# A hybrid decoder step on one core: a new opening of the head pairs, block-diagonal chunk states, late top-k rounds and a token-major last norm

## What is computed

```python
n = rmsnorm(x, norm1)
c_rw, c_att, c_gate = _split(n @ w_in, (RW_COLS, ATT_COLS, GATE_COLS))
o_rw, wkv_new, shift_new = rwkv7_mix(c_rw, shift_prev, wkv_prev, ...)
o_att = attend(q, k, v, qi, ki, wi * IDX_W_SCALE)      # top-k indexer, then softmax over the selected keys
merged = jax.nn.sigmoid(g_rw) * (o_rw @ p_rw) + jax.nn.sigmoid(g_att) * (o_att @ p_att)
h = x + merged @ w_o
f, conv_new = conv_glu(rmsnorm(h, norm2), conv_prev, w_up, conv_w, conv_b, w_down)
y = rmsnorm(h + f)                                     # after the last layer
```

## Time and profile before

| | |
|---|---|
| median of 3 runs | 1784.6 us (1784.6 to 1786.84) |
| the profiled execution's own time | 1784.55 us |
| its span, from the first to the last instruction | 1783.0 us |
| PE busy | 1762.4 us, 99% |
| DVE busy | 1119.2 us, 63% |
| ACT busy | 759.8 us, 43% |
| mean share of the DMA engines | 40 to 60% in most slices |
| granted clock of PE, mean | 0.998 |

### The profile page before, as it was taken

The page is one execution under the profiler, slowest core; times in us unless marked ns, Lnnn a source line. Parts: engine busy times, 40 slices in busy tenths (PEclk is TensorE's granted clock), DMA queues, the critical chain, the costliest instruction groups (busy, mean ns, idle before and its releaser), DMA issues.

```text
span 1783.0 us, 40707 instructions
## 1 busy us (share of the span) xinstructions
PE 1762.4 (99%) x16500; PEld 1704.9 (96%) x16500; DVE 1119.2 (63%) x1995; ACT 759.8 (43%) x1059; POOL 53.6 (3%) x103
## 2 busy tenths in 40 slices
PE   9999999999999999999999999999999999999997
PEld 8999899988888888999999999999999999999996
DVE  7764954667777777765566666666666665444444
ACT  6456444555555554433443333333333333333332
POOL 2500000000000000000000000000000000000000
PEclk9999999999999999999999999999999999999999
DMA  7644344433332333644454444444444444555553
GB/s 279 227 162 163 130 160 152 155 114 107 108 107 104 111 108 113 222 166 151 174 219 165 165 165 165 165 165 165 165 165 165 165 165 162 175 169 174 169 170 132
DMA packets 51696, 283.46 MB, mean 159 GB/s; under 512 B 7248, under 2 KB 11856, under 8 KB 25776
## 3 DMA queue, kind: packets, MB, share of 16 engines
q1 hardware_dynamic: 43632, 260.35, 41.7%
q10 hardware_dynamic: 3744, 12.56, 2.0%
q0 software_dynamic: 4256, 9.65, 1.8%
HBM read 274.26 MB, written 8.27 MB: 158 GB/s over the span
## 4 chain that ended last, share of the span: by engine, by line
PE 95%; DVE 3%; DMA 1%; ACT 0%; issue 0%; DVEq 0%; SPq 0%
PE bank L621 30%; PE bank L623 28%; PE bank L622 28%; PE bank L945 1%; PE bank L985 1%; DVE w_lo L567 1%; DVE scores L1919 1%; PE bank L852 0%; PE bank L905 0%; DVE max L1886 0%; DMA x_raw<-in_x 0%; PE bank L800 0%; PE bank L817 0%; PE bank L1046 0%; PE bank L642 0%
## 5 line engine op out<-in xcount | busy, mean ns | idle before, releaser
L621 PE MATMUL bank<-x_split,w_lo 128*128 128x288 f32 x2880 | 873.2, 303 | 3.3 <-DVE w_lo L567 2.1
L622 PE MATMUL bank<-x_split,w_hi 128*128 128x288 f32 x2880 | 849.5, 295 | 0.0
L623 PE MATMUL bank<-x_split,w_hi 128*128 128x288 f32 x2880 | 847.0, 294 | 0.0
L587 ACT ACTIVATE w_hi<-w_raw 128x2048 fp32r<-128x2048 f32 (+1 forms) x262 | 468.8, 1789 | 590.9 <-PE bank L623 578.7
L567 DVE TENSOR_TENSOR w_lo<-w_raw,w_hi 128x2048 fp32r<-128x2048 f32 (+1 forms) x238 | 503.8, 2117 | 283.7 <-ACT w_hi L587 283.4
L621 PEld LDWEIGHTS bank<-x_split,w_lo 128*128 128x128 f32 x2880 | 540.2, 188 | 20.3 <-issue 9.6
L622 PEld LDWEIGHTS bank<-x_split,w_hi 128*128 128x128 f32 x2880 | 541.0, 188 | 1.8 <-issue 0.7
L623 PEld LDWEIGHTS bank<-x_split,w_hi 128*128 128x128 f32 x2880 | 542.2, 188 | 0.0
L621 PE MATMUL bank<-act_split,w_lo 128*128 128x288 f32 x704 | 208.5, 296 | 0.0
L622 PE MATMUL bank<-act_split,w_hi 128*128 128x288 f32 x704 | 207.7, 295 | 0.0
L623 PE MATMUL bank<-act_split,w_hi 128*128 128x288 f32 x704 | 207.0, 294 | 0.0
(11 more groups left out here) (390 smaller groups left out, 1537.9 us busy)
## 6 DMA issues: line engine op xcount, KB each, us to landing
w_raw<-in_w_up SPq DMA_DIRECT2D x88, 1024.0 KB, 4.8
w_raw<-in_w_in SPq DMA_DIRECT2D x47, 1024.0 KB, 4.9
w_raw<-in_w_down SPq DMA_DIRECT2D x64, 704.0 KB, 4.0
w_raw<-in_w_gate SPq DMA_DIRECT2D x32, 1024.0 KB, 4.9
w_raw<-in_w_p SPq DMA_DIRECT2D x16, 1024.0 KB, 4.8
w_raw<-in_w_o SPq DMA_DIRECT2D x16, 1024.0 KB, 4.8
h<-in_x ACTq DMA_DIRECT2D x1, 2304.0 KB, 10.3
h_spill<-h ACTq DMA_DIRECT2D x1, 2304.0 KB, 9.6
```

Of the source, the lines that this page charges most:

```text
L587: actv(WHI[:, slot, 0:kt], WRAW[:, slot, 0:kt], ACT.Copy).then_inc(sem("w_hi"), 3 if isinstance(n, int) and n == 2 else 1)
L621: mm(out, wl, hi, start=first and k == ks[0], stop=False, skip_group_check=True)
L622: mm(out, w, lo, start=False, stop=False, skip_group_check=True)
L623: ins = mm(out, w, hi, start=False, stop=last and k == ks[-1], skip_group_check=True)
```

## The change

- **Pair opening.** The chunk matrices' products come first. The 8 transposes are cut in two groups of 4, `turned`: keys and values behind `b_mm` into bank 2, the other two into bank 6 behind the third inversion product. The `fill(5)` ahead of the first inversion product is gone; its blocks are put one by one behind later steps (`fill(4)` for `fill(3)` in three places, `fill(3 + merge)`, `fill(3)` for `fill(2)`, one more at the end).
- **State loop.** DVE writes the chunk maps (`chunk_map`, now [128, 3, 128]) and a copy of each state (`state_blocks`) as block-diagonal 128x128 matrices whose other blocks are zero, so that one product on the whole array does both heads; there are 6 of them for a pair in place of 12. The output's product is issued one step later than the state's.
- **Output centring.** PE multiplies the output by the identity less the block of means; ACT squares it and copies it; DVE's centring is gone.
- **Attention.** The 8 rounds of `late` are moved into the steps (3, 2 and 3 rounds, then the bias), and the constants are FILL_TOPK_S 33, FILL_TOPK 12, FILL_SAMPLE 16, FILL_SOFTMAX 15. The total stays 384.
- **Start.** The norm gains are sent from ACT's queue ahead of the weights; the last quarter of x is sent behind the weights of unit 2, the constants behind those of unit 3; the tables of parameters later.
- **Last norm.** The squares are the stationary operand and two columns of 1/2048 the moving one, so that the sum is one number for each token on a partition; root and reciprocal are of 128x6; three diagonal matrices bring it back over all partitions with three products of up to 128 columns. Y_PARTS is now 2, 3, 4, 4 and 3 tiles (before 4, 4, 4, 2, 2).

```diff
+    c["centre"] = eye - c["head_ones"] / HD
...
-FILL_ROPE, FILL_REQUESTS, FILL_TOPK_S, FILL_TOPK, FILL_SAMPLE = 12, 2, 25, 30, 14
+FILL_ROPE, FILL_REQUESTS, FILL_TOPK_S, FILL_TOPK, FILL_SAMPLE = 12, 2, 33, 12, 16
 FILL_DOTS = (8, 7) + (8,) * 4
-FILL_SCORES, FILL_SOFTMAX, FILL_P_T, FILL_PV = 8, 14, 5, 4
+FILL_SCORES, FILL_SOFTMAX, FILL_P_T, FILL_PV = 8, 15, 5, 4
...
-                for w, src in enumerate((BT, KTL, RKV[:, 2, :], AR[:, 0, :])):
-                    for tt in range(2):
-                        ins = tr(BK[2 + tt][:, w * P:(w + 1) * P], src[:, tt * P:(tt + 1) * P], ident)
-                ins.then_inc(sem("tok_mm"), 1)
+                settle(pe)
+
+                def turned(bank, sources):
+                    for w, src in enumerate(sources):
+                        for tt in range(2):
+                            ins = tr(BK[bank][:, (2 * tt + w) * P:(2 * tt + w + 1) * P], src[:, tt * P:(tt + 1) * P], ident)
+                    ins.then_inc(sem("tok_mm"), 1)
...
+                turned(2, (KTL, RKV[:, 2, :]))
...
-                fill(5)
...
-                pe.wait_ge(sem("tok_sb"), v)
                 pe.wait_ge(sem("block16"), v)
                 settle(pe)
-                blockwise(2, L1, U)
+                blockwise(3, L1, U)
                 fill(3)
+                pe.wait_ge(sem("tok_sb"), v * 2 - 1)
                 pe.wait_ge(sem("inv_l"), v * 8 - 7)
                 settle(pe)
-                blockwise(3, L2, UT, True)
+                blockwise(2, L2, UT, True)
                 fill(3)
                 pe.wait_ge(sem("inv_l"), v * 8 - 6)
                 settle(pe)
-                blockwise(2, L1, UT, True)
-                fill(3)
+                blockwise(3, L1, UT, True)
+                turned(6, (BT, AR[:, 0, :]))
+                fill(4)
+                pe.wait_ge(sem("tok_sb"), v * 2)
                 pe.wait_ge(sem("inv_l"), v * 8 - 5)
                 settle(pe)
-                blockwise(3, L2, T)
+                blockwise(2, L2, T)
                 pe.wait_ge(sem("sin_in"), v * 16)
...
-                    fill(3)
+                    fill(3 + merge)
...
-                fill(2)
+                fill(3)
...
+                def both_heads(banks, c, lhs, rhs):
+                    tt, par = divmod(c, 2)
+                    return mm(BK[banks[par]][:, tt * CH:(tt + 1) * CH], lhs, rhs, start=False, stop=False, skip_group_check=True)
+
                 for c in range(1, NCH):
-                    tt, par = divmod(c, 2)
                     fill(2)
+                    if c > 1:
+                        pe.wait_ge(sem("read"), v * 4 - 4 + c)
+                        both_heads(read, c - 1, STB[:, c % 2, :], QT[:, c - 1, :])
                     pe.wait_ge(sem("state"), v * 4 - 4 + c)
                     pe.wait_ge(sem("map"), v)
-                    settle(pe)
-                    for e, h in enumerate(halves):
-                        ins = grown(grow, 0, tt, MT[h, c, :], ST[h, c - 1, :], e, par)
-                    ins.then_inc(sem("state_mm"), 1)
-                    if c == 1:
-                        pe.wait_ge(sem("read"), v)
-                        settle(pe)
-                    for e, h in enumerate(halves):
-                        ins = grown(read, 0, tt, ST[h, c - 1, :], QT[h, c, :], e, par)
-                ins.then_inc(sem("y_mm"), 1)
+                    both_heads(grow, c, MTB[:, c - 1, :], ST[:, c - 1, :]).then_inc(sem("state_mm"), 1)
                 fill(2)
+                pe.wait_ge(sem("read"), v * 4)
+                both_heads(read, NCH - 1, STB[:, 0, :], QT[:, NCH - 1, :]).then_inc(sem("y_mm"), 1)
                 if not last:
                     pe.wait_ge(sem("s_grown"), v)
...
-                mm(BK[5][:, 0:N], head_ones, YS[:], start=True, stop=True).then_inc(sem("y_mean"), 1)
+                mm(BK[5][:, 0:N], centre, YS[:], start=True, stop=True).then_inc(sem("y_mean"), 1)
...
-            last_sum(2, FSUM, FSQ)
+            pe.wait_ge(sem("norm_sq_used"), KT * 2 + KT - 1)
+            for tt, t0 in enumerate(TOKEN_TILES):
...
-                act.wait_ge(sem("y_centred"), v)
-                actv(YQ[:], YS[:], ACT.Square).then_inc(sem("y_sq"), 1)
+                act.wait_ge(sem("y_mean"), v)
+                actv(YQ[:], BK[5][:, 0:N], ACT.Square).then_inc(sem("y_sq"), 1)
+                actv(YS[:], BK[5][:, 0:N], ACT.Copy).then_inc(sem("y_centred"), 1)
...
-            st.done(marks_to_bias(early, BIASP[:, 0, 0:P], causal[0]))
-            select(ACC[:, 1, :], TOPK_P, BIASP[:, 1, :], causal[1], FILL_TOPK).then_inc(sem("bias_ready"), 1)
+            marks_to_bias(early, BIASP[:, 0, 0:P], causal[0]).then_inc(sem("bias_ready"), 1)
             dve.wait_ge(sem("bias_ready"), 1)
+            streamed(FILL_TOPK)
+            late = ACC[:, 1, :]
+
+            def late_rounds(r0, r1):
+                for r in range(r0, r1):
+                    eight_best(late, TOPK_P - 8 * r)
...
+                    if which == 0:
+                        late_rounds(0, 3)
...
+                if n == 1:
+                    late_rounds(3, 5)
...
+                if n == 1:
+                    late_rounds(5, 8)
+                    st.done(marks_to_bias(late, BIASP[:, 1, :], causal[1]))
...
+                def state_blocks(c):
+                    tt, par = divmod(c, 2)
+                    for e, h in enumerate(halves):
+                        ins = V.tensor_scalar(STB[h, c % 2, e * HD:(e + 1) * HD], BK[6 + par][h, tt * CH:(tt + 1) * CH],
+                                              PC[h, c:c + 1], None, ALU.mult)
+                    ins.then_inc(sem("read"), 1)
...
-                V.tensor_tensor(MT[:, 1::2, :], grid(7, P, 2), spread(eye_ch, 1, [P, 2, CH]), ALU.add)
-                V.tensor_tensor(MT[:, 2, :], BK[6][:, P + CH:2 * P], eye_ch, ALU.add).then_inc(sem("map"), 1)
+                for e, h in enumerate(halves):
+                    V.tensor_tensor(MTB[h, 0::2, e * HD:(e + 1) * HD], BK[7][h, P:2 * P].rearrange("p (u f) -> p u f", u=2),
+                                    spread(eye_ch[h], 1, [CH, 2, CH]), ALU.add)
+                for e, h in enumerate(halves):
+                    ins = V.tensor_tensor(MTB[h, 1, e * HD:(e + 1) * HD], BK[6][h, P + CH:2 * P], eye_ch[h], ALU.add)
+                ins.then_inc(sem("map"), 1)
...
+                state_blocks(0)
                 for c in range(1, NCH):
+                    dve.wait_ge(sem("state_mm"), v * 3 - 3 + c)
+                    state(c)
+                    if c + 1 < NCH:
+                        state_blocks(c)
                     if c == 1 and not last:
                         dve.wait_ge(sem("mix_cur"), v)
                         dve.wait_ge(sem("prm"), it + 2)
                         mix_prev(it + 1, 1).then_inc(sem("rkv"), 1)
                     if c == 2 and not last:
                         mix_prev(it + 1, 0)
-                    dve.wait_ge(sem("state_mm"), v * 3 - 3 + c)
-                    state(c)
                 dve.wait_ge(sem("state_s_mm"), v)
...
-                dve.wait_ge(sem("y"), v)
-                dve.wait_ge(sem("y_mean"), v)
-                V.scalar_tensor_tensor(YS[:], BK[5][:, 0:N], -1.0 / HD, YS[:], ALU.mult, ALU.add).then_inc(sem("y_centred"), 1)
...
-            norm_rstd(2, FRSTD)
+            dve.wait_ge(sem("norm_rms"), 3)
+            st.done(V.reciprocal(FROOT[:], FROOT[:]))
```

More of the change, by code:

```diff
@@ L1665, in _ @@
             down_units(KT // 2 - 1, 2 * DU - 2)
-            norm_root(2, FRSTD)
+            act.wait_ge(sem("norm_sq_used"), KT * 3)
+            actv(FROOT[:].rearrange("p t x -> p (t x)"), BK[2][:, 0:6], ACT.Sqrt, bias=EPSC[:]).then_inc(sem("norm_rms"), 1)
             for i, k in enumerate(Y_PARTS):
@@ L2119, in pair @@
                 inv(1)
-                V.transpose(L2[:], blocks(2))
-                V.tensor_copy(U, blocks(2)).then_inc(sem("inv_l"), 1)
+                V.transpose(L2[:], blocks(3))
+                V.tensor_copy(U, blocks(3)).then_inc(sem("inv_l"), 1)
                 V.transpose(LB[:], UB[:])
```

67 lines of the change are left out of this document (47 added, 20 removed).

## The result

The changed kernel took **1814.8 us** (median of 4 runs, 1814.3 to 1815.9) against 1784.6 us before; the ratio is 1.0169, with a 95% interval of 1.0151 to 1.0186. The forecast was 1800.0 with a range of 1788 to 1806: the side was right, but half of the loss was missed and the time lies 9 us above the range.

The account below looks back on a forecast made before the run. PE was taken as the bound, with 95% of the chain. Pairs + 11.0, attention + 7.6, start - 1.5 and end - 1.8 sum to + 15.3 on some 1784.6 us: 1800.0 us, range 1788 to 1806.

Parts of the forecast that it names:

- Pairs: Pairs of heads: PE waits 2 us at block16, period 46.6 us, + 1.6 seven times, + 11.0 us.
- State loop: State loop in each pair: 6 whole-array products at 1.3 us in place of 1.7 on PE, - 0.4 us.
- the 0.03 us a pass: Whole-array products by the skill's 60-cycle minimum: 0.03 us a pass, not 0.11, pairs some 7 us cheaper; not adopted.
- Attention: Attention: old waits go, - 2.6, but changed block counts add new waits; + 7.6 us, between + 1 and + 10.
- Waits A: Attention, first step: PE waits for the low part because no split is due ahead of the exponentials, 3.6 us.
- B: Attention, second step: PE waits again because the count falls short of a split ahead of the exponentials, 3.7 us.
- D: Attention, token mixing: the split falls behind the mixing's operations and PE waits, 1.9 us.
- the smaller ones: Attention: smaller shifts of the same kind, 0 to 2 us, taken as 1.0 us.
- Start: Start: ACT's wait for unit 2's weights goes with the last quarter of x behind them, - 1.5 us.
- End: End: small forms of the last norm and a first output part of two tiles save 1.8 us.
- Centring: Output centring in the pairs: taking it from DVE gives nothing, since kk_max behind it waits for PE anyway.
- The third rival, the clock: Attention: the clock falls to 1.2 GHz, 3 us lost behind each of A and B, 1806 us; chance 0.07.

Follow-up runs that it names:

- runs 9: The kernel before with the change's opening of the pairs alone (no fill(5), blocks at the later places): 1801.9 us.
- run 1: The changed kernel with fill(5) back ahead of the first inversion product, its blocks taken from the later places: 1797.3 us.
- run 6: The changed kernel with fill(5) back, FILL_TOPK 17, norm gains on SP's queue, and DVE's mixing of the next pair's r moved out of the state loop: 1778.4 us.
- run 10: The kernel before with the new output centring alone: 1781.8 us, ratio 0.9984.
- run 13: The kernel of run 6 with the old pair opening in full (eight transposes ahead of the chunk products, fill(5)): 1776.7 us, ratio 0.9960.
- Run 4: The changed kernel with 7 identity products that compute nothing on PE ahead of the wait for block16: 1808.7 us.
- run 2: The changed kernel with FILL_TOPK 17 in place of 12, five stream blocks earlier in the attention: 1800.8 us.
- run 3: The changed kernel with the norm gains sent from SP's queue ahead of x again: 1813.1 us, ratio to before 1.0157.
- run 11: The kernel before with the last norm by tokens and the new parts of the output alone: 1783.9 us, ratio 0.9996.

## Why the prediction had the side right and half of the size

- **Pairs, + 11.0 forecast, 19.5 measured.** The mechanism stands: PE waits at `block16` for a list of DVE that got only 0.16 us shorter (1.65 us where 2.0 were forecast), and runs 9 and 1 show that the missing `fill(5)` makes it. The period without the clock was 46.75 against 46.6, 12.3 us of the 19.5. That this comes so near is partly luck: it holds a wait of 0.6 us for `state_s` that the forecast did not have (run 6 gets 0.47 of it back), against 0.14 by the new centring (run 10), and an opening whose moves, apart from the `fill(5)`, cost some 0.2 us (run 13) where 0.39 were forecast. The step that failed is the one that let PE stand for 2 us and priced nothing behind it: the low clock costs 1.45 us behind five of seven openings, 7.2 us. Run 4 leaves the wait and takes the low clock away, and its pairs give back 7.05 us.
- **State loop, - 0.4 a pair.** Right on PE: the chunks cost 0.21 + 0.44 + 0.44 + 0.16 = 1.25 us where 1.3 were forecast. Two passes of a whole-array product take 0.21 us, so the row decided rightly; the 0.03 us a pass, the prediction's estimate from a figure of the Trainium skill ("TensorEngine Tiling (Array Packing)", section "Instruction Overhead"), is not what these products cost. What I left out is DVE's side: the copies fill its idle time in the loop, `state_s` comes late, and PE waits 0.57 to 0.60 us for it. I had costed the products and not the three pairs of copies that they need.
- **Attention, + 7.6 forecast, 11.7 measured.** Waits A, B, D and the smaller ones were forecast at 3.6, 3.7, 1.9 and 1.0 and came as 3.38, 3.75, 1.56 and 1.45; run 2 shows that the counts make them. (The addends of ACT's path to A come to 11.1 and not 11.4, so A should have been 3.3.) The missing 4 us are the clock behind A and B.
- **Start, - 1.5 forecast, + 0.24 measured.** The term itself is there but half as large, 0.7 us by the means of the 100th block, and the step left out the move of the norm gains to the head of ACT's queue, ahead of the first weights, which costs 1.5 by the same means; run 3's median gives 1.7 back. I had counted the DMA that left SP's queue and not the queue that it entered. The low clock in this stretch adds nothing that can be seen at the 100th block: run 1, whose start has none, is there at 51.17 us and the change at 50.82.
- **End, - 1.8 forecast, - 1.3 measured**, 0.7 to 1.3 over all traces; by medians (run 11) it can't be told from nothing.
- **Centring, 0 forecast**: 0.9 us of gain in run 10's trace. The prediction was right that DVE's list starts no sooner behind `kk_sum`, and left out that ACT's root, which the list needs, waited behind the centring.

The misses add up: 7.2 for the clock and 1.3 for the rest of the pairs, 4.1 in the attention, 1.7 at the start and 0.5 at the end are 14.8 us, the distance from 1800.0 to 1814.8.

The third rival, the clock, was the mechanism that decided, at a chance of 0.07 and only for A and B. The argument against it was a misreading: the 1.47 us of idle time in the window of the earlier trace rows were two waits, of 0.89 and 0.57 us, and the 0.63 a third. No single wait of the kernel before was as long as those that I forecast (the longest that it has between its first block and its last sum are 1.36 us in the start and 1.13 at 701 us, with the clock at 1.00 behind both), so the rows said nothing about what 1.65 us, let alone 3.7, would do. The rival's own number, 3 us behind each of A and B, was 6 for the attention where 4 were measured, and nothing for the pairs, so its 1806 was short too. The Trainium skill ("TensorE: Matmul & The Clock Gate", section "HAM oscillation — how this bites in real kernels") describes bursts of matmuls with pauses of some 3 to 5 us between them, each burst of which then starts at the low clock. The trace agrees behind A and B (3.38 and 3.75 us); in the pairs the low clock comes at shorter pauses than in that example, 1.65 us, and not at each of them.

## What to carry to other kernels

A wait on PE has two prices: its length, and the low clock behind it. When a change is forecast to make PE wait longer than any single wait in the trace, price the clock too, and read single waits from the timeline, not from a window's sum. Where blocks between steps are counted, the count at each place is a threshold: here one constant was worth 14 us, and five blocks ahead of a wait 17. And whatever leaves one queue or engine (gains to ACT's queue, half products to copies on DVE) must be costed where it arrives.

## What the runs showed of the hardware

- A wait of PE of 0.86 us lowered the clock in none of seven openings, one of 1.27 in none (in the run profiled), one of 1.65 in five of seven (in each of the three traces that have it, the change and runs 2 and 3), one of 1.83 in six of seven, and waits of 3.38 and 3.75 us both times. Equal waits with equal work around them went both ways in one execution, so the length of the wait alone doesn't decide.
- Waits of 1.45 and 1.56 us between blocks of the stream lowered it in none of twelve cases (six traces). At the start, ahead of the first block, waits of 1.93 to 2.67 us lowered it in seven traces of eight, and waits of up to 1.61 in none. No run has a wait of 1.65 us between blocks of the stream, so whether the small products around the pairs' wait take part is not shown.
- Behind a fall PE ran some 3 us at 0.50 in the pairs and up to 6 us behind wait A, and a matmul of 288 columns started every 0.24 us in place of 0.133.
- Products that compute nothing, 14 passes in 1.5 us of waiting, kept the clock at 1.00 in all pairs and gained 6.1 us.
